# Opening reordered, dilated scores with the two heads in turn, last pair's maxima exchanged before its last unit

## The reference

```
h = rms_norm(x, g);  z = h @ w_in             # q, k, v, gate of 4 retention heads
q = rope(q, pos);  k = rope(k, pos) / 16      # needs sin and cos of pos * freq

# dilated attention: 8 heads of 64, 3 groups (window, dilation) = (128,1) (512,4) (2048,16)
s = q @ k.T / 8 + bias(bucket(distance))      # per head and group
m = max(s);  p = exp(s - m);  den = sum(p);  num = p @ v
m_all = max over the groups;  scale = exp(m - m_all)
o = sum(num * scale) / sum(den * scale);  out = o @ w_out
```

## Time and profile before

| | |
|---|---|
| median of 3 runs | 2301.42 us (2300.96 to 2301.71) |
| profiled execution | 2301.16 us |
| its span, first to last instruction | 2299.2 us |
| mean granted TensorE clock | 0.983 |
| TensorE busy | 2198.7 us, 96% |
| VectorE busy | 1185.5 us, 52% |
| ScalarE busy | 861.3 us, 37% |
| GpSimd busy | 968.7 us, 42% |

### The profile page before, as it was taken

The page is one execution under the profiler, slowest core; times in us unless marked ns, Lnnn a source line. Parts: engine busy times, 40 slices in busy tenths (PEclk is TensorE's granted clock), DMA queues, the critical chain, the costliest instruction groups (busy, mean ns, idle before and its releaser), DMA issues.

```text
span 2299.2 us, 29536 instructions
## 1 busy us (share of the span) xinstructions
PE 2198.7 (96%) x10336; PEld 1820.5 (79%) x10336; DVE 1185.5 (52%) x1714; ACT 861.3 (37%) x1264; POOL 968.7 (42%) x706
## 2 busy tenths in 40 slices
PE   6999999999999999988999999999999989999997
PEld 4888888677788888866888888887788777888885
DVE  5756546876666666667265222225455446222224
ACT  4423233454444444444444223224424434323223
POOL 4253535354433333324445445444423223455443
PEclk8999999999999999999999999999999989999998
DMA  4322222232222222222322222223211111222321
GB/s 147 92 97 74 97 83 85 84 128 93 74 73 73 76 85 77 78 78 90 112 74 92 105 96 91 94 107 110 91 56 63 67 55 44 103 91 91 109 92 55
DMA packets 37838, 200.03 MB, mean 87 GB/s; under 512 B 4331, under 2 KB 9707, under 8 KB 15372
## 3 DMA queue, kind: packets, MB, share of 16 engines
q1 hardware_dynamic: 28496, 188.76, 23.2%
q10 hardware_dynamic: 9276, 10.37, 1.4%
HBM read 193.87 MB, written 5.24 MB: 87 GB/s over the span
## 4 chain that ended last, share of the span: by engine, by line
PE 85%; DVE 9%; ACT 2%; DVEq 2%; issue 1%; DMA 0%; SPq 0%; ACTq 0%
PE bank L415 16%; PE bank L416 15%; PE bank L419 15%; PE bank L402 12%; PE bank L403 12%; PE bank L404 12%; ACT WH L991 1%; DVE PKL L1552 1%; DVE X L1770 1%; DVE T L1768 1%; DVE SS L1571 1%; DVE R L1560 1%; DVE T L1697 1%; DVE HL L1566 1%; DVE MYL L1552 0%
## 5 line engine op out<-in xcount | busy, mean ns | idle before, releaser
L354 POOL TENSOR_TENSOR WL<-RAW,WH 128x512 fp32r<-128x512 f32 x700 | 965.0, 1410 | 1301.6 <-ACT WH L991 1301.6
L991 ACT ACTIVATE WH<-RAW 128x2048 fp32r<-128x2048 f32 (+1 forms) x181 | 335.9, 1856 | 643.9 <-PE bank L404 321.5
L415 PE MATMUL bank<-HH,WH 128*128 128x512 f32 x968 | 389.2, 402 | 9.2 <-DVEq L2209 5.9
L416 PE MATMUL bank<-HL,WH 128*128 128x512 f32 x968 | 381.4, 394 | 0.0
L419 PE MATMUL bank<-HH,WL 128*128 128x512 f32 x968 | 239.2, 389 | 0.0
L415 PEld LDWEIGHTS bank<-HH,WH 128*128 128x128 f32 x968 | 184.4, 191 | 51.8 <-DVEq L2209 6.4
L416 PEld LDWEIGHTS bank<-HL,WH 128*128 128x128 f32 x968 | 184.4, 190 | 39.7 <-issue 2.2
L419 PEld LDWEIGHTS bank<-HH,WL 128*128 128x128 f32 x968 | 181.7, 188 | 37.8
L2056 DVE TENSOR_TENSOR X<-X,bank 128x512 f32<-128x512 f32 x128 | 87.6, 687 | 196.7 <-PE bank L419 117.4
L402 PE MATMUL bank<-HH,WH 128*128 128x512 f32 x352 | 138.4, 393 | 17.6 <-POOL WL L354 11.7
L2047 DVE SCALAR_TENSOR_TENSOR TG<-bank,RS 128x512 f32<-128x512 f32 x64 | 44.0, 688 | 205.1 <-PE bank L404 135.8
(11 more groups left out here) (410 smaller groups left out, 4464.9 us busy)
## 6 DMA issues: line engine op xcount, KB each, us to landing
RAW<-panels SPq DMA_DIRECT2D x175, 1024.0 KB, 4.8
X<-xin SPq DMA_DIRECT2D x4, 512.0 KB, 9.2
xsave<-X ACTq DMA_DIRECT2D x4, 512.0 KB, 2.8
X<-xsave ACTq DMA_DIRECT2D x1, 2048.0 KB, 8.3
TAB<-scratch ACTq DMA_DIRECT2D x16, 128.0 KB, 2.8
out<-ACC SPq DMA_DIRECT2D x8, 256.0 KB, 2.5
RS<-decay ACTq DMA_DIRECT2D x4, 256.0 KB, 2.4
scratch<-O SPq DMA_DIRECT2D x4, 256.0 KB
```

Of the source, the lines that this page charges most:

```text
L354: gp.tensor_tensor(WL[:, s, cs], RAW[:, s, cs], WH[:, s, cs].bitcast(f32), ALU.subtract).then_inc(lo_ready, 1)
L415: nc.tensor.matmul(o, wh[:, columns[k - k0]], xh[:, k, :], start=first and k == k0, stop=False)
L416: nc.tensor.matmul(o, wh[:, columns[k - k0]], xl[:, k, :], start=False, stop=False)
L991: return nc.scalar.activation(dst, src, ACT.Copy)
```

## The change

It has three parts. In the opening, the first panel's two tiles take a new order: all high-weight products slice by slice, then the low-weight products. VectorE's reciprocal of RC is issued between the first and the second range step of the angles. In the dilated attention `att_scores` issues each product for the first head and then for the second, so that neighbours on the queue lie in different halves of the rows; the signals of both heads go with the last product of each. For the last pair, the exchange of the maxima is issued before unit 8, VectorE's biases before the scaling of unit 8, and ScalarE's first exponentials before the copy of the values of group 1, behind the panel split.

```
+            def tiles_low_last(os, w, width, xh, xl, nk, wait):
+                wh, wl = w[:2]
+                pe.wait_ge(hi_ready, w[2] + 1)
+                columns = [[slice(k * width + i * 128, k * width + i * 128 + 128) for i in range(len(os))] for k in range(nk)]
+                for k in range(nk):
+                    wait(k)
+                    for i, o in enumerate(os):
+                        nc.tensor.matmul(o[:, :], wh[:, columns[k][i]], xh[:, k, :], start=k == 0, stop=False)
+                        nc.tensor.matmul(o[:, :], wh[:, columns[k][i]], xl[:, k, :], start=False, stop=False)
+                for k in range(nk):
+                    for i, o in enumerate(os):
+                        low_up_to(w, columns[k][i].start)
+                        end = nc.tensor.matmul(o[:, :], wl[:, columns[k][i]], xh[:, k, :], start=False, stop=k == nk - 1)
+                return end
...
-                tiles_together([bank(4), bank(5)], w, 256, HH, HL, KD, wait_h)[1].then_inc(panel_used, 1)
+                tiles_low_last([bank(4), bank(5)], w, 256, HH, HL, KD, wait_h).then_inc(panel_used, 1)
...  att_scores
-                for e in range(2):
-                    rows = slice(64 * e, 64 * e + 64)
...
-                        end = mm3(o, DQH[rows, par, qs], DQL[rows, par, qs], DKH[rows, par, ks], DKL[rows, par, ks], True, True)
-                    end.then_inc(S["dil_s_made"], 1)
+                for r in range(4):
...
+                    for j, (q, k) in enumerate(((DQH, DKH), (DQH, DKL), (DQL, DKH))):
+                        for e in range(2):
+                            rows = slice(64 * e, 64 * e + 64)
+                            end = nc.tensor.matmul(os_[e][which][:, at], q[rows, par, qs], k[rows, par, ks],
+                                                   start=j == 0, stop=j == 2)
+                            if r == 3 and j == 2:
+                                end.then_inc(S["dil_s_made"], 1)
...  TensorE, dilated attention
                 if n > 0:
                     att_weighted(c, 2)
+                if n == ATT_PAIRS - 1:
+                    exchange_maxima(n)
                 unit(n, 8)
                 value_transposes(n, 1)
...
-            exchange_maxima(last)
             value_transposes(last, 2)
...  ScalarE
                     panel_behind(n, 8)
+                if n == ATT_PAIRS - 1:
+                    exponentials(n, 0)
                 high_values(n, 1)
...
-            exponentials(last, 0)
             high_values(last, 2)
...  VectorE, opening
+            def inverse_columns_of_pre0():
+                ve.wait_ge(S["norm_root"], NORMS.index("pre0") + 1)
+                v.reciprocal(RC[:, :], RC[:, :]).then_inc(free[1], 1)
+                ve.drain().then_inc(S["cols_ready"], 1)
...
                 less(t[0], t[0], 1.0 / turns, _parts(turns, 7, 6))
+                between()
                 less(t[2], t[0], 1.0 / TWO_PI, _parts(TWO_PI, 8, 5))
...
-            angles(SIN1[:, :].bitcast(i32), FREQ1, [ACC[:, j, :] for j in range(4)])
-            ve.wait_ge(S["norm_root"], NORMS.index("pre0") + 1)
-            v.reciprocal(RC[:, :], RC[:, :]).then_inc(free[1], 1)
-            ve.drain().then_inc(S["cols_ready"], 1)
+            angles(SIN1[:, :].bitcast(i32), FREQ1, [ACC[:, j, :] for j in range(4)], inverse_columns_of_pre0)
...  VectorE, dilated attention
                     result(c)
+                if n == ATT_PAIRS - 1:
+                    biases(n)
                 scaled_unit(n, 8)
                 low_values(n, 1)
...
-            biases(last)
             low_values(last, 2)
```

More of the change, by code:

```diff
@@ L826, in att_scores @@
                 par = (3 * n + g) % 2
-                for e in range(2):
-                    rows = slice(64 * e, 64 * e + 64)
-                    if g == 0:
-                        os_ = [bank(2 + 2 * e), bank(3 + 2 * e)]
-                    else:
[L832 to L842, removed]
-                        end = mm3(o, DQH[rows, par, qs], DQL[rows, par, qs], DKH[rows, par, ks], DKL[rows, par, ks], True, True)
-                    end.then_inc(S["dil_s_made"], 1)
+                os_ = [[bank(2 + 2 * e), bank(3 + 2 * e)] if g == 0 else [bank(2 + e)] for e in range(2)]
+                for r in range(4):
+                    qs = slice(128 * r, 128 * r + 128)
+                    if g > 0:
+                        which, at, ks = 0, qs, qs
+                    elif r == 0:
+                        which, at, ks = 0, slice(0, 128), qs
+                    elif r == 1:
+                        which, at, ks = 0, slice(128, 384), slice(0, 256)
+                    else:
+                        which, at, ks = 1, slice(256 * r - 512, 256 * r - 256), slice(128 * r - 128, 128 * r + 128)
+                    for j, (q, k) in enumerate(((DQH, DKH), (DQH, DKL), (DQL, DKH))):
[5 more added lines that the diff above has]
+                                end.then_inc(S["dil_s_made"], 1)
             def exchange_maxima(n):
@@ L1584, in scaled, with angles @@
                         lo(dl[:, k - 1, :], T[:, (k - 1) % 2, :], dh[:, k - 1, :]).then_inc(S[sig], 1)
-            def angles(positions, freq, t):
+            def inverse_columns_of_pre0():
+                ve.wait_ge(S["norm_root"], NORMS.index("pre0") + 1)
+                v.reciprocal(RC[:, :], RC[:, :]).then_inc(free[1], 1)
+                ve.drain().then_inc(S["cols_ready"], 1)
+            def angles(positions, freq, t, between):
                 MAGIC = 1.5 * 2.0 ** 23
```

## The result

The changed kernel takes 2276.43 us (median of 4 runs, 2274.16 to 2276.95), the kernel before 2301.56 beside it (4 runs, 2300.96 to 2301.71): ratio 0.989, 95% interval 0.9874 to 0.9905. The forecast was 2281.6 in 2274 to 2289. The profiled execution is the fastest of the four: 2274.16, span 2272.1, mean granted clock 0.989. Against the profiled one of the kernel before that is 27.0 us, where the medians differ by 25.1. In what follows, before and after name these two profiled executions.

The account below looks back on a forecast made before the run. TensorE was taken to bound the kernel, carrying 85% of the chain that ended last. Opening 9.8 plus scores 11.0 less 1.2 for the maxima made 19.6 off the profiled 2301.16: 2281.6 us, range 2274 to 2289.

Parts of the forecast that it names:

- low halves last: First panel in the opening: low-weight products after the high ones let TensorE start earlier; 0.5 us sooner (0 to 1.0).
- opening: From the start to V's last product: earlier inverse columns and fewer half-clock products; 9.8 us saved (bounds 7 and 13).
- scores: Dilated attention: alternating heads run two products per slot, 1.0 us a block over 11 blocks; 11.0 us (bounds 8 and 12).
- last pair's maxima: Tail: exponentials start sooner, but the copy of V and first output tile come 3.8 later; a loss of 1.2 us.
- clock elsewhere: Half-clock stretches outside the opening, as in the third pair's last unit: taken as 0, between 4 gained and 3 lost.
- Inverse columns: Opening: reciprocal between the range steps brings the RC transposition to 36.4 instead of 43.90, 7.5 us sooner (6.7 to 7.8).
- The clock of the opening: Small matrices before V: clock falls in mid-stretch, so about 1.9 of 2.8 us saved, plus 0.4 on V's products.
- rival A: The clock holds in the opening: 12.7 us gained for 9.8, total 2278.7; chance 0.30.
- The sines: Opening: VectorE's rotation starts about 9 us sooner, at 45.5, ends near 59, and V at 62 to 66 covers it.
- B: Scores: alternating gives nothing because one head's weight load holds up the other; total 2292.6, chance 0.09.
- D: Scores: each change of head costs 0.10 us, 28.8 more, with no sharing; total 2321.4, slower; chance 0.03.
- C: The first head cannot use the time, K or a panel behind GpSimd being late; half the opening lost, 2286.5; chance 0.08.

Follow-up runs that it names:

- opening_only: The kernel before with only both opening parts, the first panel's low-weight products last and the reciprocal between the range steps: 2288.28 us, ratio 0.9932.
- mended_again: Repeat of the changed kernel with DKL before the first pair's first logits and the last pair's panel split behind exponentials and copy: 2265.74 us.
- dkl_early: The changed kernel, with VectorE making DKL before the logits of the first block in the first pair: 2271.42 us, ratio 0.9878.
- maxima_only: The kernel before with only the last pair's maxima, biases and first exponentials moved: 2300.82 us, ratio 0.999.
- no_maxima: The changed kernel without the part on the last pair's maxima, so opening and scores only: 2277.32 us, ratio 0.9895.
- both_mended: The changed kernel with DKL before the first pair's first logits and the last pair's panel split behind exponentials and copy: 2265.81 us, ratio 0.9857.
- inverse_only: The kernel before with only the reciprocal moved between the range steps, first panel in its old order: 2288.09 us, ratio 0.9952.
- scores_only: The kernel before with only the heads alternating at every product in the scores: 2289.48 us, ratio 0.9947.
- triples: The kernel before with scores in turns of three products of one head, then three of the other: 2290.04 us, ratio 0.9953.
- changed_again: The changed kernel timed once more, same code: 2276.39 us, ratio 0.9898.

## Why the prediction came out as it did, step by step

The forecast of 2281.6 is 5.2 above the median of 2276.43 and 7.4 above the profiled execution of after, which lies at the very edge of the range (2274.16 for 2274). The sum was made from the profiled execution of before. By terms, forecast and read:

| term | forecast | read in after |
|---|---|---|
| low halves last | 0.5, inside the opening | nothing that can be told |
| opening | 9.8 | 13.0 |
| scores | 11.0 | 9.1 |
| last pair's maxima | -1.2 | +1.0 with the clock of the tail; +0.6 to +0.9 by leaving it out and by doing it alone |
| clock elsewhere | 0 | 3.9 |

**Low halves last: no gain, and the floor was laid at the wrong slice.** I took VectorE's last slice of HL as what sets the end. It came at 11.78 + 7.01 = 18.79, so that floor was 23.3, but panel 1 starts at 24.27. TensorE takes the last slice only at 19.74, without a wait. It waits once, at 16.86, for the fifth slice (15.03 + 1.78 = 16.81); from there 16 high and 16 low products follow without a gap, 32 x 0.23 = 7.4, to 24.27. The early start went into products at half clock (11 at half pace where before 7) and into that wait. x also came later than before by 0.48 (ScalarE's first wait for it ends at 11.03 for 10.55), but it comes between 10.55 and 11.21 in all traces, with either order.

**Inverse columns: right in kind and time.** 36.4 forecast, 36.10 measured. I had added 0.6 for a stretched reciprocal and 0.9 for one more slowed operation of the first step. Neither came: six operations in 5.45, as before, one of them slowed. GpSimd's panel did not move with TensorE's first product: it starts at 32.94 for 32.74.

**The clock of the opening: the first term that was mis-sized, 9.8 for 13.0.** I took a fall in the middle of the small matrices. They ran at 1.00, in 3.76 us, and V behind them too. My reason was the row where such work did not raise the clock. That showed work at half clock that left it there, and I read it as work that lowers it. The opening was rival A's, 12.7, and the row says 13.0. The runs also show that it is no certainty: opening_only and mended_again lose one stretch there. The Trainium skill's rule that I weighed ("TensorE: Matmul & The Clock Gate", "Why this matters for your kernels") gave 12.7. The seven traces that hold the clock here agree with it. The two that lose it there speak against it, and so does the first pair, where the clock falls behind a wait of 2.02 in all six traces that have this wait, and in none of the three in which it is taken away.

**The sines: right in order, wrong in time.** The rotation starts at 47.52, not at 45.5: V's start and ScalarE's copies were early as forecast, but from 41.57 on GpSimd's next panel meets VectorE's second step. Its five operations take 5.59 where before they took 4.66, the two behind them 1.36 and 1.58 for 0.43 and 0.69, and sine and cosine wait for these two. The cover held, but with less room than I had: K's low half ends near 60.9, V at 61.52. With a faster V this would be the next wait.

**Scores: right in kind and in the price of a block; 9.1 for 11.0 by the clock.** A slot for two products, 0.95 for a block of groups 1 and 2 and 1.04 for group 0 against my 1.0. The bound of 12 would have needed the first pair's block. That one was given back to VectorE's DKL, as forecast, the wait going from 0.98 to 2.02. What I didn't see is what the longer wait brings: a stretch at half clock, worth 1.6, without which the term would be 10.7. dkl_early has both back. Rivals B and D are out (and C: neither K nor GpSimd is late): the head changes at every product and costs nothing, and so the rule that I weighed ("TensorEngine Tiling (Array Packing)", "Tiling Modes" in the Trainium skill) has no case in this change of halves.

**Last pair's maxima: mechanism right, price wrong.** The output tile is later, by 3.7 in maxima_only against before and by 3.75 in after against no_maxima, as worked out. But I priced the transposes at half clock (3.0) and the second tile between 2.1 and 3.8. In both traces the stretch at half clock ends with the first tile: 1.5 for the transposes and 2.2 for the second tile. The part then gains 0.6 to 0.9, at the edge of my bound of 0.6 gained or just past it.

**Clock elsewhere: the second term that was mis-sized, 0 for 3.9.** I took it at nothing, with 4 gained as a bound, because all of it moves in time. The row of 14 slow products from which I priced it is the fourth pair's; the third's is like it (the row in the section on the result). The gain is no luck of the profiled execution, since it goes with the scores through all traces. From the third pair's last block of scores to the fourth pair's first block it is 43.56 to 43.69 in the four traces with the old scores, and 39.99 to 40.03 in seven of the nine with the new ones; the block gives 0.95 of this, and 2.7 is the stretch at half clock that is gone. (In dkl_early and both_mended it is 41.6, with 3.4 us at half clock.) From the last block to the output tile it is 26.51 to 26.59 in before, inverse_only and opening_only, and 24.43 to 24.45 in scores_only, triples and no_maxima: 0.95 and 1.2. TensorE waits the same 1.99 to 2.00 ahead of the third pair's last unit in all thirteen traces, so the length of that wait does not decide it. Why the clock holds there with the new scores stays open.

What was luck in the profiled execution is in the first and second pair, where it has 3.4 us at half clock and changed_again has 6.8. The misses lie mostly on one side: the opening gave 3.2 more than forecast, the clock elsewhere 3.9 and the maxima 2.2, and only the 1.9 of the scores go the other way.

## What to carry to other kernels

When an edit takes time from the engine that bounds, look at once for the next wait it runs into, and price it twice: as itself, and with the clock that may fall behind it (here 2.1 us of waiting cost 3.7 to 5.2). Where an instruction is moved up an engine's order, move the whole chain that its successor needs: the exponentials behind the split gained under 1 us, ahead of it 5.8 more. Before a change of clock is called luck, compare the same place in all traces with the edit and without it. And read a row of the clock for what it shows: work that leaves a low clock low is not shown to lower a high one.

## What the runs showed of the hardware that I had not expected

- Products on the two halves of the rows run two to a slot (0.111 us with 128 columns) even when three of one half stand on the queue ahead of three of the other: 1.49 a block in both orders.
- The granted clock behind the same instructions differs from run to run: in the opening 1.00 in seven traces and one stretch of 3.4 us at 0.50 in two, and behind the wait for DKL 3.4 us in four and 6.8 us in two. With it the same code takes 2274.15 to 2281.92.
- The clock can change with the edit where the wait does not: ahead of the third pair's last unit TensorE waits 1.99 to 2.00 in all traces, and behind it 6.8 us are at 0.50 in the four with the old scores, none in seven and 3.4 us in two with the new ones.
- VectorE's range operations take 0.69 alone (one every 0.77) and 1.6 where GpSimd's subtractions run beside them: of the five in 5.59, three took 0.69 and two 1.6.
